# Inverse levels of a gated DeltaNet: an earlier start, other work between their steps, and sample products grouped by tile shape

## What is computed

```python
L = jnp.where(strict, beta[..., None] * kk * decay, 0.0)
A = L + jnp.eye(T)
rhs = [v * beta, k * beta * exp(gc)]
u, w = triangular_solve(A, rhs)             # unit lower triangular
v_new = u - w @ S
o = (q * exp(gc)) @ S + (q k^T * decay) @ v_new
S_new = S * exp(g_last) + (k * exp(g_last - gc))^T @ v_new
```

## Time and profile before

| what | value |
|---|---|
| runs of the kernel | 954.7, 955.31, 955.76 us, median 955.31 us |
| the profiled execution's own time | 955.39 us |
| its span on the core | 953.7 us |
| PE busy | 937.7 us of the span, 98% |
| DVE, ACT, POOL busy | 68%, 47%, 18% |
| DMA moved | 103.69 MB, mean 109 GB/s |
| granted TensorE clock | 1.00 of full speed in every slice |

### The profile page before, as it was taken

The page is one execution under the profiler, slowest core; times in us unless marked ns, Lnnn a source line. Parts: engine busy times, 40 slices in busy tenths (PEclk is TensorE's granted clock), DMA queues, the critical chain, the costliest instruction groups (busy, mean ns, idle before and its releaser), DMA issues.

```text
span 953.7 us, 16664 instructions
## 1 busy us (share of the span) xinstructions
PE 937.7 (98%) x6807; PEld 848.9 (89%) x6807; DVE 647.9 (68%) x1083; ACT 451.9 (47%) x836; POOL 169.7 (18%) x198
## 2 busy tenths in 40 slices
PE   9999999999989999999999999999999999999998
PEld 8899888998868877889888999999999999888887
DVE  7627888776676455661665999999999999435321
ACT  6634454648466335463664345444444446333310
POOL 0061101104654241000001042222222220000000
PEclk9999999999999999999999999999999999999999
DMA  8624243221104066043822422222222223413221
GB/s 299 230 80 144 69 154 90 71 70 46 45 4 134 2 225 213 14 164 115 321 96 66 177 91 89 82 77 75 81 86 90 89 89 124 172 45 110 67 99 55
DMA packets 73820, 103.69 MB, mean 109 GB/s; under 512 B 2577, under 2 KB 53905, under 8 KB 73361
## 3 DMA queue, kind: packets, MB, share of 16 engines
q1 hardware_dynamic: 73744, 102.63, 32.2%
HBM read 92.27 MB, written 10.35 MB: 108 GB/s over the span
## 4 chain that ended last, share of the span: by engine, by line
PE 89%; DVE 5%; ACT 3%; issue 1%; POOL 1%; DMA 1%; SPq 0%; ACTq 0%; DVEq 0%; POOLq 0%
PE bank L1198 8%; PE bank L1199 8%; PE bank L1200 8%; PE bank L533 7%; PE bank L535 7%; PE bank L534 7%; PE bank L495 6%; PE bank L497 5%; PE bank L496 5%; PE bank L463 4%; PE bank L559 2%; PE bank L561 2%; PE bank L560 2%; PE bank L588 1%; PE bank L483 1%
## 5 line engine op out<-in xcount | busy, mean ns | idle before, releaser
L2141 DVE TENSOR_TENSOR wlo<-wraw,whi 128x2048 fp32r<-128x2048 f32 (+1 forms) x56 | 126.1, 2252 | 103.8 <-ACT whi L1591 94.5
L1591 ACT ACTIVATE whi<-wraw 128x2048 fp32r<-128x2048 f32 (+1 forms) x58 | 109.3, 1885 | 100.0 <-PE bank L535 72.9
L495 PE MATMUL bank<-hhi,whi 128*128 128x320 f32 x352 | 116.1, 330 | 0.0
L497 PE MATMUL bank<-hhi,wlo 128*128 128x320 f32 x352 | 108.7, 309 | 0.0
L496 PE MATMUL bank<-hlo,whi 128*128 128x320 f32 x352 | 108.7, 309 | 0.0
L495 PEld LDWEIGHTS bank<-hhi,whi 128*128 128x128 f32 x352 | 66.2, 188 | 4.7 <-issue 3.8
L496 PEld LDWEIGHTS bank<-hlo,whi 128*128 128x128 f32 x352 | 66.2, 188 | 2.8 <-issue 2.2
L497 PEld LDWEIGHTS bank<-hhi,wlo 128*128 128x128 f32 x352 | 66.1, 188 | 0.0
L533 PE MATMUL bank<-whi,hhi 128*128 128x512 f32 x150 | 58.4, 389 | 0.0
L534 PE MATMUL bank<-wlo,hhi 128*128 128x512 f32 x150 | 58.4, 389 | 0.0
L535 PE MATMUL bank<-whi,hlo 128*128 128x512 f32 x150 | 58.3, 389 | 0.0
(11 more groups left out here) (489 smaller groups left out, 2684.3 us busy)
## 6 DMA issues: line engine op xcount, KB each, us to landing
wraw<-in_w_in SPq DMA_DIRECT2D x13, 1024.0 KB, 5.3
wraw<-in_w_gate SPq DMA_DIRECT2D x11, 1024.0 KB, 5.2
wraw<-in_w_up SPq DMA_DIRECT2D x11, 1024.0 KB, 5.2
wraw<-in_w_down SPq DMA_DIRECT2D x10, 1024.0 KB, 5.1
kTs<-in_cache_sb_k SPq DMA_DIRECT2D x8, 512.0 KB, 4.5
vraw<-in_cache_sb_v SPq DMA_DIRECT2D x8, 512.0 KB, 5.0
wraw<-in_w_mix_out SPq DMA_DIRECT2D x4, 1024.0 KB, 6.0
kmT<-in_cache_mem_k SPq DMA_DIRECT2D x8, 512.0 KB, 6.1
```

The lines of the kernel that those rows point to most:

```text
L495: T.matmul(o, wh[:, k, cs], hhi[:, k, hs], start=(k == 0), stop=False)
L497: ins = T.matmul(o, wl[:, k, cs], hhi[:, k, hs], start=False, stop=(k == KD - 1))
L1591: V(wv(whi, i), wv(wraw, i), ACT.Copy).then_inc(s["w_hi_ready"], 1)
L2141: V.tensor_tensor(wv(wlo, i), wv(wraw, i), wv(whi, i).bitcast(F32), ALU.subtract)\
```

## The change

- `HALF_FILLS` are now six half units, behind steps 1, 3, 6, 9, 12 and 15; the fill between the last beta rows and the loop is gone. There are still twelve units.
- `turn_vk(0)` moves from the last level into the loop, behind step 18. DVE's products of it go ahead of item 17 (`v_part(0)`) and item 18 (`k_part(0)`), so block 0 now counts first in `kd_ready`.
- ACT's `blocks_out(PT)` goes behind its copies of items 0 and 1. POOL makes the masks of items 4 and 5 ahead of the samples' starting inverse, and clears XT behind the mask of item 15. DVE's readings of sB (`gate_yb`) follow their units.
- The last level becomes one staggered sequence: in step n, X of block n, Y of block n - 2 and dX of block n - 4, head by head. ACT's copies follow that order.
- In `sample_new` and `sample_out` the four full products come first, then all the narrow ones; only the first product of a bank carries `start`.

```diff
@@ -421,7 +421,8 @@
         LAG = 2
-        HALF_FILLS = (1, 7, 12, 17)
+        HALF_FILLS = (1, 3, 6, 9, 12, 15)
+        KEYS_TURNED = 18
@@ -816,7 +817,6 @@
                 beta_rows(i)
-            fill()
             pe.wait_ge(s["silu_done"], 12)
@@ -858,34 +858,44 @@
                     half_fill()
+                if n == KEYS_TURNED:
+                    turn_vk(0)
...
             upper, lower = half64(0), half64(1)
-            for i in range(PT):
-                evacuated(pe, ("dX", LEVELS - 2, i))
-                b = take(("X", LEVELS - 2, i))
+            def last_products(x=None, y=None, d=None):
+                if x is not None:
+                    evacuated(pe, ("dX", LEVELS - 2, x))
+                    bx = packed(take(("X", LEVELS - 2, x)))
+                if y is not None:
+                    evacuated(pe, ("X", LEVELS - 2, y))
+                    by = packed(take(("Y", LEVELS - 1, y)))
+                if d is not None:
+                    evacuated(pe, ("Y", LEVELS - 1, d))
+                    bd = packed(take(("dX", LEVELS - 1, d)))
                 for h in range(HEADS):
-                    ins = T.transpose(packed(b)[upper, h, :], XT[i][upper, h, upper], ident[upper, upper])
-                done(ins, ("X", LEVELS - 2, i))
-            turn_vk(0)
-            for i in range(PT):
-                evacuated(pe, ("X", LEVELS - 2, i))
-                b = take(("Y", LEVELS - 1, i))
-                for h in range(HEADS):
-                    ins = T.matmul(packed(b)[lower, h, :], LT[i][upper, h, lower], Xb[i][upper, h, :], start=True, stop=True)
-                done(ins, ("Y", LEVELS - 1, i))
-            for i in range(PT):
-                evacuated(pe, ("Y", LEVELS - 1, i))
-                b = take(("dX", LEVELS - 1, i))
-                for h in range(HEADS):
-                    ins = T.matmul(packed(b)[upper, h, :], Xb[i][lower, h, :], XT[i][lower, h, lower], start=True, stop=True)
-                done(ins, ("dX", LEVELS - 1, i))
+                    if x is not None:
+                        last_x = T.transpose(bx[upper, h, :], XT[x][upper, h, upper], ident[upper, upper])
+                    if y is not None:
+                        last_y = T.matmul(by[lower, h, :], LT[y][upper, h, lower], Xb[y][upper, h, :], start=True, stop=True)
+                    if d is not None:
+                        last_d = T.matmul(bd[upper, h, :], Xb[d][lower, h, :], XT[d][lower, h, lower], start=True, stop=True)
+                if x is not None:
+                    done(last_x, ("X", LEVELS - 2, x))
+                if y is not None:
+                    done(last_y, ("Y", LEVELS - 1, y))
+                if d is not None:
+                    done(last_d, ("dX", LEVELS - 1, d))
+            for n in range(PT + 4):
+                last_products(x=n if n < PT else None, y=n - 2 if 2 <= n < PT + 2 else None, d=n - 4 if n >= 4 else None)
...
                 evacuated(pe, ("dX", (LEVELS if i < PT else SAMPLE_LEVELS) - 1, i))
-                pe.wait_ge(s["kd_ready"], 1 if i == PT else i + 2)
+                pe.wait_ge(s["kd_ready"], 2 if i == PT else 1 if i == 0 else i + 2)
                 b = take(("wT", i))
@@ -904,7 +914,7 @@
                         ins = T.matmul(bank[b][r, h * P:(h + 1) * P], left[:, b2, h, r], stS[:, 2 * p + b2, h, :],
-                                       start=False, stop=(b2 == 1))
+                                       start=False, stop=(b2 == 1), skip_group_check=True)
                 return ins
@@ -913,7 +923,9 @@
                 for h in range(HEADS):
-                    T.matmul(bank[b][:, h * P:(h + 1) * P], XT[PT][:, h, :], smp_v[:, h, :], start=True, stop=False)
+                    T.matmul(bank[b][:, h * P:(h + 1) * P], XT[PT][:, h, :], smp_v[:, h, :], start=(h == 0), stop=False,
+                             skip_group_check=True)
+                for h in range(HEADS):
                     ins = by_sample(b, h, apart_w)
@@ -922,7 +934,9 @@
                 for h in range(HEADS):
-                    T.matmul(bank[b][:, h * P:(h + 1) * P], qkD[PT][:, h, :], smp_vn[:, h, :], start=True, stop=False)
+                    T.matmul(bank[b][:, h * P:(h + 1) * P], qkD[PT][:, h, :], smp_vn[:, h, :], start=(h == 0), stop=False,
+                             skip_group_check=True)
+                for h in range(HEADS):
                     ins = by_sample(b, h, apart_q)
@@ -1506,6 +1520,10 @@
                     decays(i + 1)
+                else:
+                    filled(pool, ("brow", PT))
+                    for n in range(PT, PT + 2):
+                        level_mask(n)
                 pool.wait_ge(s["lb_ready"], i + 1)
@@ -1514,9 +1532,9 @@
                     level_mask(i)
-            for n in range(PT, len(LM_ORDER)):
+            for n in range(PT + 2, len(LM_ORDER)):
                 level_mask(n)
-                if n == LM_RING - 1:
+                if n == 15:
                     for j in range(NT):
@@ -1848,9 +1866,10 @@
             cut_hi(B_OUT[0][0])
-            blocks_out(PT)
-            for l, i in LM_ORDER:
+            for n, (l, i) in enumerate(LM_ORDER):
+                if n == 2:
+                    blocks_out(PT)
                 b = filled(e, ("Y", l, i))
@@ -1860,12 +1879,13 @@
             upper, lower = half64(0), half64(1)
-            for i in range(PT):
-                b = filled(e, ("X", LEVELS - 2, i))
-                V(Xb[i][upper, :, :], packed(b)[upper, :, :], ACT.Copy).then_inc(bank_free[b], 1)
-            for i in range(PT):
-                b = filled(e, ("Y", LEVELS - 1, i))
-                V(Xb[i][lower, :, :], packed(b)[lower, :, :], ACT.Copy, scale=-1.0).then_inc(bank_free[b], 1)
+            for n in range(PT + 2):
+                if n < PT:
+                    b = filled(e, ("X", LEVELS - 2, n))
+                    V(Xb[n][upper, :, :], packed(b)[upper, :, :], ACT.Copy).then_inc(bank_free[b], 1)
+                if n >= 2:
+                    b = filled(e, ("Y", LEVELS - 1, n - 2))
+                    V(Xb[n - 2][lower, :, :], packed(b)[lower, :, :], ACT.Copy, scale=-1.0).then_inc(bank_free[b], 1)
             e.wait_ge(s["apart_zero"], 1)
@@ -2408,28 +2428,41 @@
-            def vk_part(i):
+            def vk_slots(i):
+                return (smp_v, smp_kb, smp_kd) if i == PT else (scr[i % 2], scr[2 + i % 2], scr[4 + i % 2])
+            def v_part(i):
                 b = filled(dve, ("Vt", i))
-                slots = (smp_v, smp_kb, smp_kd) if i == PT else (scr[i % 2], scr[2 + i % 2], scr[4 + i % 2])
                 if 2 <= i < PT:
                     filled(dve, ("dS", i - 2))
-                V.tensor_tensor(slots[0][:, :, :], quad(b), spread(beta[:, i, :], 2, [P, HEADS, P]), ALU.mult)\
+                V.tensor_tensor(vk_slots(i)[0][:, :, :], quad(b), spread(beta[:, i, :], 2, [P, HEADS, P]), ALU.mult)\
                     .then_inc(bank_free[b], 1)
+            def k_part(i):
+                slots = vk_slots(i)
                 b = filled(dve, ("Kt", i))
...
-            gate_yb(0, 0)
+            def vk_part(i):
+                v_part(i)
+                k_part(i)
             for n, (l, i) in enumerate(LM_ORDER):
+                if n == 3:
+                    gate_yb(0, 0)
                 if n == PT:
...
                     gate_yb(0, 1)
-                if n == 18:
+                if n == 14:
                     gate_yb(1, 0)
+                if n == KEYS_TURNED - 1:
+                    v_part(0)
+                if n == KEYS_TURNED:
+                    k_part(0)
                 b = filled(dve, ("dX", l, i))
@@ -2443,7 +2476,6 @@
             gate_yb(1, 1)
-            vk_part(0)
             for i in range(PT):
```

## The result

The changed kernel takes 958.2 us (median of 8 runs, 957.41 to 959.43) against 955.16 us for the kernel before (8 runs): a ratio of 1.0031, 95% interval 1.0022 to 1.004. It is slower by 3.0 us, above the forecast of 952.6 and above its range. The profiled execution took 957.56 us.

The account below looks back on a forecast made before the run. PE's own work was taken to bound the kernel (busy 937.7 of 953.7 us). Loop -0.1, last level -0.5 and samples -2.2 gave -2.8 against 955.39: 952.6 us, range 951.2 to 955.0.

Parts of the forecast that it names:

- Start of the loop: Before the level loop: step 0 starts at 255.1 without the fill; masks and moved copies delay nothing, costed at nothing.
- The loop: Level loop: ends at 287.6 instead of 287.7 with one fill and the turn inside, a gain of 0.1 us.
- the forecast's own sign of being wrong: Level loop: the forecast is wrong if the loop is longer than 32.5 us from 255.1.
- The new wait: Loop, ahead of step 21: PE waits for DVE to free the bank of block 0's key product, 1.2 us lost.
- Last level: Staggered X, Y and dX: first X to first w product 5.8 us instead of 6.3, a gain of 0.5.
- The bound, a loss of 0.2 us: Last level: the worst case, if groups of a step run one after the other.
- The clock is 1.00 throughout, so it enters nowhere: Whole kernel: the clock, 1.00 throughout the profile, was given no part in the count.
- Sample products: Sample groups: full products first, then narrow ones, 2.8 us each instead of 3.9; 2.2 us gained in all.
- Grouping does nothing: Rival, sample products: narrow products wait on something other than tile shape, so the 2.2 us stay; 954.8 us, chance 0.12.
- the bank wait does not bite: Rival, loop at step 21: DVE is ahead of the count, so 1.2 us less; 951.4 us, chance 0.13.
- Code comes late: Rival, loop behind the turn: one instruction-issue stall again, 1.2 us more; 953.8 us, chance 0.18.
- The slower rival: Loop: code comes late in every dense stretch, six stalls of 1.2 us cost 7.2; 959.8 us, chance 0.07.

Follow-up runs that it names:

- the banks' experiment: Sixth experiment: changed kernel with plain last level, the outputs of the turn (still in the loop) moved to banks 0 and 1; 951.04 us, ratio 0.9957.
- ninth experiment: Changed kernel, still woven, with the turn of block 0 out of the loop and ahead of step 4 of the last level; 956.06 us, ratio 1.0013.
- the fifth: Changed kernel with the plain last level and the turn of block 0 back between X and Y; 952.37 us, ratio 0.997.
- third experiment: Kernel before with the sample products grouped, nothing else; 953.43 us, ratio 0.9979.
- fourth: Kernel before with the woven last level alone, the turn of block 0 ahead of it; 961.59 us, ratio 1.0061.
- tenth experiment: Changed kernel, woven last level kept, with the turn's outputs in banks 0 and 1; 956.07 us, ratio 1.0009.
- eighth experiment: Changed kernel with the staggered last level ordered by kind in each step and the turn's outputs in banks 0 and 1; 951.46 us, ratio 0.9961.

## Why the prediction was wrong

*Start of the loop*: right. Step 0 at 255.00, and neither masks nor `blocks_out(PT)` held a step.

*The loop*: right in mechanism and nearly in size. It ends at 287.93 (287.6 forecast). From step 0 that is 32.93 us, so the forecast's own sign of being wrong, a loop over 32.5 us, was met; the sign left no room above the count itself (287.6 - 255.1). The new wait stands ahead of step 21 on the key product. The trace shows 1.85 us of idle time there; the loss is what goes with it, 1.12 us by the banks' experiment (1.2 forecast). What the forecast had not seen is that this idle stretch can take the clock down as well.

*Last level*: **the step that failed**, in the words "two groups on different tiles should take 0.5 together, as a step of the loop does four quarters in 0.5". That row was of products alone. Where the group on the other tile is a row of transposes, woven head by head, a step takes 1.72 us. Steps 4 and 5, of Y and dX, overlap as forecast (step 4 in the changed kernel's timeline runs from 296.62 to 297.15), so the rule was right for one kind of work and was carried to a mixture that no row showed. By the forecast's count step 2 to step 5 was 2.3 us (1.6, and half of 1.4); it took 297.76 - 293.47 = 4.29. The bound, a loss of 0.2 us, was for groups one after the other. It holds for that: by kind, where they do run so, the level takes 6.0 us, less than 6.33 + 0.2. Woven it takes 8.58, since the alternation is slower than one group after the other, a case that the bounds did not have. The forecast's own count also had the weave lose against the plain order without saying so: 6.33 less the turn is 5.3, and 5.8 was forecast.

The Trainium skill ("TensorEngine Tiling (Array Packing)", Key Properties) says that different tiles load and multiply in parallel, and that a change of tiling mode drains TensorE. The first holds here for products (e.g. 0.62 us for a step of X and Y as matmuls) and not for transpose beside matmul; the second agrees with the sample groups (3.90 us with eight changes of tile shape, 2.77 with two). All instructions of the weave have the same 64x64 tiles, so neither sentence covers its 0.43 us a head.

*"The clock is 1.00 throughout, so it enters nowhere"*: the second error. It was a fact of one profiled execution, taken for a constant: of the 61 runs of the kernel before beside the experiments, three have a mean clock below 0.999 (957.33 and 957.63 us with 0.998, 957.78 us with 0.949). Behind the weave the clock is at 0.50 for some 6.8 us. The two steps of dX take 1.79 us there, and from the first w to the first sample product it is 311.77 - 301.04 = 10.73 us against 307.38 - 298.38 = 9.00 in the kernel with the grouping alone: 1.7 us, which is the whole of what lacks behind the level. Of the 3.3 us that the level is longer than in plain order, 0.7 are the stagger by itself (6.0 by kind less 5.3), some 0.8 the clock (17 instructions of dX in 1.79 us, where the plain order has 29 in 1.70, so 17 in 1.0), and the remaining 1.8 the alternation, near the two steps' own 3.44 - 1.87 = 1.6. So of the 5.0 us about half is the clock, by these rows of single executions; the ninth experiment's two runs at full clock, 2.0 us above the fifth, fit that.

*Sample products*: right. 2.8 us forecast, 2.77 measured; 1.8 of 2.2 us by the medians.

*Rivals*: "Grouping does nothing" and "the bank wait does not bite" are refuted. "Code comes late" did not occur in the changed kernel. Issue gaps did come back in others: in step 7 of the old loop with 0.61 us (third experiment) and 1.16 (fourth) for the 0.88 of before, and near 284.25 with 0.45 us in the fifth and ninth, the loops without the turn, where seven steps stand in a row. So the gap goes with the order of the work and its length varies; no run here shows what it waited for. The Trainium skill ("Runtime: NRT & Kernel Launch", Instruction fetch mechanics) holds the fetch of a further block of instructions for mostly hidden; whether these gaps are such fetches is open. The slower rival had the right sign by a mechanism that did not take place. The true mechanism was in none.

## What to carry to other kernels

Before two streams of small products are woven, look for a row in which exactly these kinds alternate; overlap seen between matmuls says nothing about a transpose beside a matmul, and a group by kind is the safe order. When an edit makes a stretch thinner for PE, price the work behind it at half the clock as one end of the range. And when an output moves ahead in a ring of banks, follow the ring to its next user: here another ring for two outputs was worth 1.7 us, and makes the best of these kernels, 951.04 us.

## What was unexpected of the hardware

- A transpose and a matmul of 64x64 float32 in turns take 0.43 us a head (one transpose, two records of the product); grouped by kind 0.22 to 0.25; with the transpose done as a matmul 0.16 (0.62 for four).
- The granted clock fell to its lower level in or behind 3.2 us of such alternation in all 24 runs of three kernels (changed, fourth and tenth experiment), and in 10 of 12 with the turn put behind it. Behind an idle stretch of 1.85 us alone it fell in some runs only (mean clock of 0.998 or less in 1 of 5 with the plain level, 4 of 11 by kind and 6 of 11 with X as a matmul). In the fifth, sixth and eighth experiment, with neither, the mean clock was 0.999 to 1.0 and the runs of a kernel lay within 0.6 us.
- The same program took 954.3 to 959.5 us as the clock's fall varied (the turn inside the weave). In the profiled executions the clock was down for some 6.8 us in the changed kernel (298.0 to 304.8) and 10.2 in the fourth experiment (298.3 to 308.5). What decides how long it lasts is open: no run changed it by itself.
- Open too: what inside PE makes the alternation slow. The runs show that it needs both kinds in turns, and no more.
